# Mixer turn edge: all sums of squares in one TensorE slot, decay formed at the turn's end, Gram products of k with k signalled apart

## The reference, cut to what matters

```python
q = _l2norm(q) * (DN_DK ** -0.5)          # x * rsqrt(sum(x*x) + eps) over 128 channels
k = _l2norm(k)
decay = where(tri, exp(where(tri, g[:, None] - g[None, :], 0)), 0)
kb, vb = k * beta, v * beta
L = where(strict, (kb @ k.T) * decay, 0)
sol = triangular_solve(L + eye(C), concat([vb, kb * exp(g)]))
attn = where(tri, (q @ k.T) * decay, 0)
# then chunk by chunk: v_new, o and the state S; at the end
o = _rmsnorm(o, dn_norm_w) * silu(z)
```

## Time and profile before

| what | value |
| --- | --- |
| time, median of 3 runs | 4238.58 us (4237.28 to 4242.46) |
| profiled execution, its own time | 4242.22 us |
| its span | 4240.3 us |
| mean granted clock of TensorE | 0.953 |
| TensorE busy over the span | 3691.2 us, 87% |
| mixer, turns 1 to 7 | about 470 to 1329 us of the span |
| last turn | about 1329 to 1440 us of the span |

### The profile page before, as it was taken

How to read it: one execution, slowest core, us unless ns; L and a number is a source line. 1 busy time by engine, 2 the same in 40 slices (tenths; PEclk the granted TensorE clock), 3 DMA queues, 4 the chain that set the end, 5 groups by cost and what they waited for, 6 DMA issues and landing times. The chain is left out here.

```text
span 4240.3 us, 66262 instructions
## 1 busy us (share of the span) xinstructions
PE 3691.2 (87%) x24298; PEld 3423.3 (81%) x24298; DVE 3024.4 (71%) x4791; ACT 1471.0 (35%) x1882; POOL 2050.7 (48%) x1144
## 2 busy tenths in 40 slices
PE   6876999999997898997679999999999898898986
PEld 3335988888896797997578888999898888888886
DVE  4777655566655214898978777778878888888886
ACT  5665444434442113222332332333332322223222
POOL 2333222222224233334047676777777767676772
PEclk9997999999998898998999999999999999999998
DMA  7991222222222123222589999999999999999994
GB/s 301 347 345 66 87 81 85 75 81 79 75 66 100 53 101 114 74 78 92 174 317 401 397 415 396 402 408 418 414 401 405 412 396 418 403 409 416 406 413 169
DMA packets 256208, 1090.68 MB, mean 257 GB/s; under 512 B 25352, under 2 KB 78856, under 8 KB 176392
## 3 DMA queue, kind: packets, MB, share of 16 engines
q1 hardware_dynamic: 170512, 543.60, 34.6%
q0 software_dynamic: 73728, 536.90, 30.9%
q10 hardware_dynamic: 11776, 7.52, 0.6%
HBM read 1047.54 MB, written 40.40 MB: 257 GB/s over the span
## 5 line engine op out<-in xcount | busy, mean ns | idle before, releaser
L248 POOL TENSOR_TENSOR wlo<-raw,whi 128x1024 fp32r<-128x1024 f32 x551 | 1344.4, 2443 | 1333.5 <-ACT whi L244 1328.2
L244 ACT CAST whi<-raw 128x1024 fp32r<-128x1024 f32 x670 | 699.1, 1049 | 1285.2 <-DMA raw<-in_u 535.1
L2099 PE MATMUL gps<-chi,whi 128*128 128x320 f32 x2048 | 656.7, 321 | 110.5 <-DVE outacc L2228 80.9
L263 PE MATMUL gps<-hi_d,whi 128*128 128x320 f32 x2048 | 653.2, 319 | 92.7 <-DVE wlo L253 61.9
L2099 PE MATMUL gps<-chi,wlo 128*128 128x320 f32 x2048 | 645.8, 315 | 0.0
L2099 PE MATMUL gps<-clo,whi 128*128 128x320 f32 x2048 | 645.7, 315 | 0.0
L263 PE MATMUL gps<-lo_d,whi 128*128 128x320 f32 x2048 | 643.6, 314 | 0.0
L263 PE MATMUL gps<-hi_d,wlo 128*128 128x320 f32 x2048 | 643.2, 314 | 0.0
L2186 DVE SCALAR_TENSOR_TENSOR dps<-ring,coef,dps 128x2048 f32<-128x2048 f32 x252 | 591.8, 2348 | 4.7 <-DVE dps L2186 0.9
L2173 DVE CUSTOM_DVE_ANT_0 ring<-ring,dps 128x2048 f32<-128x2048 f32 x256 | 582.2, 2279 | 0.0
L280 PE MATMUL gps<-act_hi,whi 128*128 128x288 f32 x2080 | 477.2, 311 | 37.9 <-POOL act_lo L511 9.0
(11 more groups left out here) (384 smaller groups left out, 5906.6 us busy)
## 6 DMA issues: line engine op xcount, KB each, us to landing
raw<-in_u SPq DMA_DIRECT2D x256, 512.0 KB, 10.5
raw<-in_v SPq DMA_DIRECT2D x256, 512.0 KB, 8.6
wada<-in_w_ada SPq DMA_DIRECT2D x96, 1024.0 KB, 6.6
raw<-in_w_in SPq DMA_DIRECT2D x96, 512.0 KB, 3.4
gateD<-gst SPq DMA_DIRECT2D x8, 2560.0 KB, 9.9
gate<-gateD SPq DMA_DIRECT2D x32, 640.0 KB, 13.5
raw<-in_w_out SPq DMA_DIRECT2D x32, 512.0 KB, 3.7
raw<-in_w_q SPq DMA_DIRECT2D x32, 512.0 KB, 3.8
```

What stands on the lines that cost most here:

```text
L244: act.copy(whi[:, k.slot, :], raw_of(k)).then_inc(W.hi, 1)
L248: pool.tensor_tensor(wlo[:, k.slot, :], raw_of(k), whi[:, k.slot, :].bitcast(F32), ALU.subtract).then_inc(W.lo, 1)
L263: m = pe.matmul(gps[:, bank, 0:DT], w, x[:, kt, :], start=(kt == 0 and n == 0), stop=(kt == KT - 1 and n == 2))
L2099: m = pe.matmul(gps[:, 2 + dt, 0:DT], w[:, slot, cols], x[:, buf, c, :], start=(c == 0 and n == 0), stop=(c == NG - 1 and n == 2))
```

## The change

All three sums of squares of an edge are made in slot 47: ScalarE squares q and k of head `h` in slot 41, and `o` into `kgd`; TensorE makes 12 products of 144 columns into `sums`, a view of the four PSUM banks `dps` (q and k first); ScalarE takes one Ln of q and k, one of `o`, then Exp of both, then Exp of the decay, then the Silu of v. The exponents of the decay are formed by VectorE in slot 46, and masked in slot 3. VectorE's slot 3 signals k times beta, now in `lt`, by `kprod` before it goes on with q and `kgd`. TensorE makes the four prompt tiles of k with `lt` in slot 4, behind `kprod`, and the other Gram products and transposes in slot 5, behind `prod`. ScalarE copies `ktok` in slot 6 and `tm` in slot 9; TensorE's transposes of `um` stand in slot 7. `qg`, `nkq` and v times beta follow `uinit` on VectorE. VectorE's wait for the store of `o` stands in slot 14.

```diff
 # TensorE
-                            if e == 3 and B:
-                                pe.wait_ge(S.sq, g + 1)
-                                for n in range(2):
-                                    for th in range(2):
-                                        m = pe.matmul(dps[:, 2 * n + th, 0:HT], ones[:, :],
-                                                      sqs[:, n, th * HT:(th + 1) * HT], start=True, stop=True)
-                                m.then_inc(S.nrm, 1)
-                            if e == 9 and B:
+                            if e == 4 and B:
+                                pe.wait_ge(S.kprod, g + 1)
+                                for t in range(NCH):
+                                    c = slice(t * CH, (t + 1) * CH)
+                                    m = pe.matmul(dps[:, 0, c], kc[:, c], lt[:, c], start=True, stop=True)
+                                m.then_inc(S.kgram, 1)
+                            if e == 5 and B:
                                 pe.wait_ge(S.prod, g + 1)
...
-                                    pe.matmul(o[0], kc[:, c], kb[:, c], start=True, stop=True)
-                                    pe.matmul(o[1], kc[:, c], qc[:, c], start=True, stop=True)
-                                    m = pe.transpose(o[2], kgd[:, c], ident)
+                                    pe.matmul(o[0], kc[:, c], qc[:, c], start=True, stop=True)
+                                    m = pe.transpose(o[1], kgd[:, c], ident)
...
-                            if e == 12 and B:
+                            if e == 7 and B:
                                 pe.wait_ge(S.uinit, g + 1)
...
-                                for th in range(2):
-                                    m = pe.matmul(dps[:, th, 0:HT], ones[:, :], sqs[:, 0, th * HT:(th + 1) * HT],
+                            if e == 47 and A:
+                                pe.wait_ge(S.sq, h + 1)
+                                for n in range(2):
+                                    for c in range(4):
+                                        m = pe.matmul(sums[:, c, 1 + n, :], ones[:, :], sqs[:, n, c * NW:(c + 1) * NW],
+                                                      start=True, stop=True)
+                                m.then_inc(S.nrm, 1)
+                            if e == 47 and B:
+                                for c in range(4):
+                                    m = pe.matmul(sums[:, c, 0, :], ones[:, :], kgd[:, c * NW:(c + 1) * NW],
                                                   start=True, stop=True)
                                 m.then_inc(S.onrm, 1)
 # ScalarE
-                            if e == 0 and B:
-                                ch(act.activation(sqs[:, 0, :], qc, ACT.Square))
-                                act.activation(sqs[:, 1, :], kc, ACT.Square).then_inc(S.sq, 1)
...
+                            if e == 41 and A:
+                                if B:
+                                    act.wait_ge(S.prod, g + 1)
+                                ch(act.activation(sqs[:, 0, :], qc, ACT.Square))
+                                act.activation(sqs[:, 1, :], kc, ACT.Square).then_inc(S.sq, 1)
...
                             if e == 47 and B:
                                 act.wait_ge(S.onrm, g + 1)
-                                for th in range(2):
-                                    ch(act.activation(sqs[:, 1, th * HT:(th + 1) * HT], dps[:, th, 0:HT], ACT.Ln,
-                                                      bias=eps[:, :], scale=1.0 / P))
-                                act.activation(sqs[:, 1, :], sqs[:, 1, :], ACT.Exp, scale=-0.5).then_inc(S.oinv, 1)
                             if e == 47 and A:
+                                act.wait_ge(S.nrm, h + 1)
+                                ch(act.activation(sqs[:, :, :].rearrange("p n (c w) -> p c n w", w=NW), sums[:, :, 1:3, :],
+                                                  ACT.Ln, bias=eps[:, :]))
+                            if e == 47 and B:
+                                ch(act.activation(kgd[:, :].rearrange("p (c w) -> p c w", w=NW), sums[:, :, 0, :],
+                                                  ACT.Ln, bias=eps[:, :], scale=1.0 / P))
+                            if e == 47 and A:
+                                act.activation(sqs[:, :, :], sqs[:, :, :], ACT.Exp, scale=-0.5).then_inc(S.invn, 1)
+                            if e == 47 and B:
+                                act.activation(kgd[:, :], kgd[:, :], ACT.Exp, scale=-0.5).then_inc(S.oinv, 1)
+                            if e == 47 and A:
+                                act.wait_ge(S.mind, h + 1)
+                                ch(act.activation(dec[:, 0:NCH, :], dec[:, 0:NCH, :], ACT.Exp))
+                                act.activation(dec[0:TS, NCH, 0:TS], dec[0:TS, NCH, 0:TS], ACT.Exp).then_inc(S.expd, 1)
                                 silu(e2, 2, S.cvv)
 # VectorE, slot 3
                                 dve.wait_ge(S.invn, g + 1)
-                                dve.wait_ge(S.o_out, g * 16 + 16)
                                 ch(tt(kc, kc, sqs[:, 1, :], ALU.mult))
+                                tt(lt[:, :], kc, rows[:, 1, :], ALU.mult).then_inc(S.kprod, 1)
                                 ch(stt(qc, qc, float(P) ** -0.5, sqs[:, 0, :], ALU.mult, ALU.mult))
-                                ch(tt(kb[:, :], kc, rows[:, 1, :], ALU.mult))
                                 tt(kgd[:, :], kc, rows[:, 3, :], ALU.mult).then_inc(S.prod, 1)
                                 dve.wait_ge(S.prod, g + 1)
-                                ch(stt(nkeg[:, :], kb[:, :], -1.0, eg, ALU.mult, ALU.mult))
+                                ch(stt(nkeg[:, :], lt[:, :], -1.0, rows[:, 2, :], ALU.mult, ALU.mult))
+                                dve.wait_ge(S.expd, g + 1)
+                                ch(tt(dec[:, 0:NCH, :], dec[:, 0:NCH, :], over4(const[:, C_INCL:C_INCL + CH]), ALU.mult))
...
 # VectorE, slot 9
+                                dve.wait_ge(S.kgram, g + 1)
+                                ch(tt(tiles4(lt[:, 0:TP]), tiles4(dps[:, 0, :]), d4, ALU.mult))
+                                ch(tt(tiles4(um[:, 0:TP]), tiles4(lt[:, 0:TP]), over4(const[:, C_LEVEL:C_LEVEL + P]), ALU.mult))
+                                ch(tt(tiles4(um[:, 0:TP]), over4(ident), tiles4(um[:, 0:TP]), ALU.subtract))
+                                dve.wait_ge(S.gram, g + 1)
...
+                                tt(um[0:TS, TP:T], const[0:TS, 0:TS], um[0:TS, TP:T], ALU.subtract).then_inc(S.uinit, 1)
                                 ch(tt(qg[:, :], qc, eg, ALU.mult))
...
+                                dve.wait_ge(S.evz, g + 1)
                                 tt(vc, vc, rows[:, 1, :], ALU.mult).then_inc(S.prod2, 1)
...
+                            if e == 46 and A:
+                                dve.wait_ge(S.rowsl, h * 16 + 16)
+                                for t in range(NCH):
+                                    ch(ts(dec[:, t, :], rows[:, 0, t * CH:(t + 1) * CH], gcol[:, bass.ds(h, 1), t],
+                                          0.0, ALU.subtract, ALU.min))
...
-                                ch(stt(kb[:, :], kb[:, :], dnw, sqs[:, 1, :], ALU.mult, ALU.mult))
+                                ch(stt(kb[:, :], kb[:, :], dnw, kgd[:, :], ALU.mult, ALU.mult))
```

More of the change, by code:

```diff
@@ L50 @@
 PACK = 5 * CW + 4 * NB * PL + 2 * P + NB
-ACT_STEPS_A_TURN = 27
-DVE_STEPS_A_TURN = 80
+ACT_STEPS_A_TURN = 23
+DVE_STEPS_A_TURN = 79
 LOW = -3.0e38
@@ L755, in build @@
             S.conv_out, S.prod2 = sems(c3, "p3_conv_out", "p3_prod2")
-            spent_outs = range(S.mix.num, S.prod2.num + 1)
+            S.kprod, S.kgram = sems(c3, "p3_kprod", "p3_kgram")
+            spent_outs = range(S.mix.num, S.kgram.num + 1)
             NL = LEVELS - 1
             SLOTS = 48
+            NW = T // 4
+            sums = dps[:, :, 0:3 * NW].rearrange("p c (n w) -> p c n w", w=NW)
             def do_turns(eng, body, sem=None, total=None, steps=0):
@@ L1209, in body @@
                             if e == 3 and B:
-                                dve.wait_ge(S.rowsl, g * 16 + 16)
-                                for t in range(NCH):
-                                    ch(ts(dec[:, t, :], rows[:, 0, t * CH:(t + 1) * CH], gcol[:, bass.ds(g, 1), t],
-                                          0.0, ALU.subtract, ALU.min))
-                                ts(dec[0:TS, NCH, 0:TS], rows[0:TS, 0, TP:T], gcol[0:TS, bass.ds(g, 1), NCH],
-                                   0.0, ALU.subtract, ALU.min).then_inc(S.mind, 1)
@@ new lines, in body @@
+                                dve.wait_ge(S.expd, g + 1)
+                                ch(tt(dec[:, 0:NCH, :], dec[:, 0:NCH, :], over4(const[:, C_INCL:C_INCL + CH]), ALU.mult))
+                                ch(tt(dec[0:TS, NCH, 0:TS], dec[0:TS, NCH, 0:TS], const[0:TS, C_SINCL:C_SINCL + TS],
+                                      ALU.mult))
+                            if e == 9 and B:
```

(17 more changed lines are left out.)

42 lines of the change are left out of this document (8 added, 34 removed).

## The result

The changed kernel takes 4184.6 us (median of 4, 4180.2 to 4193.9) against 4238.4: a ratio of 0.9874, 95% interval 0.9856 to 0.9893. It is faster by 54 us.

The account below looks back on a forecast made before the run. TensorE sets the pace, busy 115 of 123 us; gains of 3.6 (turn 1), 12.5 (turns 2 to 6), 5.9 (turn 7) and 12 (last turn) sum to 34.0, from 4238.6 to 4205 us, range 4191 to 4214 (chance 0.70).

Parts of the forecast that it names:

- the times up to um at the edge: Edge between turns, from the sums' start: o's inverse at 8.3, k's product 12.25, slot 4 at 12.55, uinit at 21.8 us.
- no fall of the clock in turn 7: Turn 7, straight code: granted clock at 1.00 after the change, where 0.60 and 0.61 stood before; turn's gain 5.9 us.
- slot 14 then held by the mixed inputs: Last turn: slot 14 some 19 us sooner, but its projection needs inputs loaded behind o's store; 12 us gain taken.
- the page's drain: ScalarE's edge: the skill page adds 1.38 us per table switch, putting o's inverse at 9.7 instead of 8.3.
- None of the rivals: Edge chain late: 4211 us (0.12); wait only moved: 4225 (0.09); slower: 4247 (0.04); little change: some 4232 (0.05).
- The Ln load itself lies before the wait, as it does now: ScalarE's edge after the change: the logarithm's table load, costing 1.28 us, is done ahead of the wait for the sums.
- four table loads for one edge: ScalarE's edge before the change: Ln and Exp for o, Ln and Exp again for q and k, Silu between.
- What comes behind the mixer starts after a block that ends for all engines, so the gain is kept: End of the sum: code behind the mixer adds no gain or loss, so the mixer's 34.0 us stands.
- the steady turn: Turns 2 to 6: waits of 4.5 us before, 1.7 + 0.1 + 0.2 after; 2.5 us gained each, 12.5 together.
- the four waits: TensorE in turns 2 to 6: squares 0.7, Gram products 2.44, transposes 1.1, convolution of x 0.3; 4.5 us go.
- k's product: Edge, VectorE: signalled at t = 12.25, needed by slot 4 at 12.55; cover 0.3 us, 0.1 us a turn charged.
- the transposes wait: Slot 7, about t = 20.2: GpSimd's subtractions hold two VectorE operations, uinit at 21.8, wait 1.7 us instead of 1.1.

## Why the prediction was wrong

What the change does at the edge was right nearly step by step: the times up to um at the edge to 0.3 us, two table loads for logarithm and exponential, no wait at the sums, no fall of the clock in turn 7, the first transposes of the last turn at t = 18 and slot 14 then held by the mixed inputs. On the page's drain: the Trainium skill, "ScalarE: Activation LUTs", section "What ACT_TABLE_LOAD costs", adds 1.38 us to each load; here the operation behind a load of 1.28 starts 0.02 us after it (590.61, 591.91), so the row decides. None of the rivals came. One reading of the edge was wrong, at a price of 0.3 us: "The Ln load itself lies before the wait, as it does now". In the kernel before it did (586.84, with the sums from 588.50); in the changed one it stands at 590.61, behind the sums of q and k. And "four table loads for one edge" does not count that of Silu, which the same sentence names: with it the trace of before has five, that of after three.

**The step that failed** is the last of the sum, "What comes behind the mixer starts after a block that ends for all engines, so the gain is kept". It took unchanged code for unchanged time. The change lengthens TensorE's program, and a loop behind it was no longer loaded again at each return: 15 us, measured both ways. The row was there to read: TensorE stood three times 4 us for issue in the kernel before, and the page counts the instruction packets. These rows lie behind the mixer, where the prediction read none. The Trainium skill, "Runtime: NRT & Kernel Launch", section "Instruction fetch mechanics", says that code comes in blocks of 16 KiB (256 instructions), that TensorE holds 2,048 instructions, and that a taken branch whose target isn't in the current window of two such blocks forces a fetch. The packets of 16 KB agree with it; nine to a return is one more than the eight blocks that a loop of 1,611 instructions touches from 224 past a border. The window of two blocks doesn't fit TensorE here, where a loop of 1,611 instructions returns without a load at five places.

**The term that was too small** is the steady turn, 2.5 us instead of 3.84. Idle time fell from 7.86 to 4.36 us: the four waits took 4.5 with them as forecast, and k's product costs nothing where 0.1 was charged. But the transposes wait 0.9 on average (1.16 at the edge shown) instead of 1.7, since slot 7 comes 0.7 us later than reckoned (t = 20.9). Busy time fell by 0.4 where 0.2 of loss was charged. Counted from each record to the start of the next, that loss is there: the sums take 0.11 us more a turn, the products of k and the transposes 0.06. The projection's products take 0.46 less. They are the same products, but the profile counts the last one ahead of a stop at its whole length (0.29 us against a step of 0.13), and three of the four stops are gone. So this part is idle time as well, as far as the modelled ends tell.

Times five the steady turn gave 6.7 us more than forecast, turns 0 and 1 gave 1.4 more, turn 7 0.3, the last turn 0.9 less. 34.0 and these 7.5 are the mixer's 41.4 within rounding. With the 15.0 of the loop they are 56.4; the stage ahead took 4.9 us more and the rest behind the mixer 3.2 more, drift the other way, which leaves the span's 48.3.

The range failed with the step: it had bounds for every unknown cost inside the mixer and none for the 2,800 us behind it.

## What to carry to other kernels

Before a gain is booked, look at the returns of the long loops behind the edit: a wait for issue of some microseconds at each return, with packets on the instruction queue, is code being loaded again, and an edit far ahead can start or stop it. The test is cheap: shift the loop by some instructions in idle time and count the packets, since the time also holds the filling (some 13 us for 184 instructions here). When two parts of an edit leave the same chain, measure them in all four combinations; here each alone gave little or lost in the loop, and the part that looked like the point (early products) cost half a microsecond a turn.

## What was not expected of the hardware

- Returns of TensorE's expert loop cost 4 us each in one place of the program and 0.2 in others; the mixer's longer loop costs some 1.5 us a turn and nine instruction packets at each of the three places tried.
- A stop of TensorE of 3.0 us was followed by some 13 us at the lower clock (granted 0.63 and 0.67), in turns of 126.3 us; one of 2.7 was followed by none, in a turn of 121.2 us.
- GpSimd's subtraction holds VectorE's small operations as hard as large ones: a 64x64 product of two SBUF tiles takes 2.26 us instead of 0.22.
- A table load of ScalarE ran while TensorE was still at the sums that its next operation needs: of 1.28 us only 0.3 showed.
